# Hybrid decoder layer on one core: the last block pair of the second FFN and the final norm worked by token halves

## The reference, cut to what matters

```python
def rms_norm(x, gain):
    y = x * lax.rsqrt(jnp.mean(x * x, axis=-1, keepdims=True) + EPS)
    return y * gain
# one layer; x is (1, 512, 1024), D_FF is 2816
x = x + 0.5 * gate1 * swiglu(modulate(rms_norm(x, g0), ...), ffn1_w_in, ffn1_w_down)
x = x + gate2 * (merged @ w_out)        # merged: two chunked gated linear attentions
h = modulate(rms_norm(x, g2), ...)
gate, up = jnp.split(h @ ffn2_w_in, 2, axis=-1)
x = x + 0.5 * gate3 * ((silu(gate) * up) @ ffn2_w_down)
return rms_norm(x, final_norm)
```

## Time and profile before

| | us |
|---|---|
| median of 3 runs | 1282.38 (1280.68 to 1282.44) |
| the profiled execution | 1284.87 |
| its span, first to last instruction | 1283.1 |
| PE busy | 1229.7 (96%) |
| DVE, ACT, POOL busy | 600.7, 415.4, 86.4 |
| last matmul of the last pair ends, from the span's start | about 1269.1 |
| first output store issued | 1276.37 |

### The profile page before, as it was taken

How to read it: one execution, slowest core, us unless ns; L and a number is a source line. 1 busy time by engine, 2 the same in 40 slices (tenths; PEclk the granted TensorE clock), 3 DMA queues, 4 the chain that set the end, 5 groups by cost and what they waited for, 6 DMA issues and landing times.

```text
span 1283.1 us, 15169 instructions
## 1 busy us (share of the span) xinstructions
PE 1229.7 (96%) x6099; PEld 1017.7 (79%) x6099; DVE 600.7 (47%) x714; ACT 415.4 (32%) x442; POOL 86.4 (7%) x121
## 2 busy tenths in 40 slices
PE   3699999999999999999999999999999999999996
PEld 2578888888878997877887788888988888888885
DVE  6855555556343657566645233345523232332231
ACT  4522222222222355544344322233422222222222
POOL 5100000000000043022320000000000000000000
PEclk7799999999999999999999999999999999999998
DMA  9275556545352422121221133233222223222211
GB/s 379 67 244 172 180 172 196 191 157 168 123 180 99 132 66 66 36 64 36 66 66 45 55 99 99 94 103 99 66 81 93 88 98 98 98 90 87 94 58 65
DMA packets 119789, 143.40 MB, mean 112 GB/s; under 512 B 3892, under 2 KB 102336, under 8 KB 119744
## 3 DMA queue, kind: packets, MB, share of 16 engines
q1 hardware_dynamic: 119560, 142.69, 34.0%
q10 hardware_dynamic: 184, 0.07, 0.0%
HBM read 140.65 MB, written 2.10 MB: 111 GB/s over the span
## 4 chain that ended last, share of the span: by engine, by line
issue 49%; PE 37%; DVE 7%; ACT 3%; DMA 3%; POOL 1%; SPq 0%; ACTq 0%; POOLq 0%; DVEq 0%
PE PS L478 10%; PE PS L480 10%; PE PS L479 10%; PE PS L682 3%; DVE ACC L1300 2%; ACT WH L873 1%; PE PS L608 1%; PE PS L521 1%; DMA RAW<-in_ffn_w_down_dram 1%; DMA RAW<-in_w_in_mix_dram 1%; PE PS L523 1%; PE PS L522 1%; DMA RAW<-in_ffn_w_in_dram 1%; DVE WL L1200 1%; PE PS L722 1%
## 5 line engine op out<-in xcount | busy, mean ns | idle before, releaser
L478 PE MATMUL PS<-HH,WH 128*128 128x512 f32 (+1 forms) x1064 | 416.0, 391 | 7.4 <-DVE HL L1222 4.4
L480 PE MATMUL PS<-HH,WL 128*128 128x512 f32 (+1 forms) x1064 | 407.9, 383 | 0.0
L479 PE MATMUL PS<-HL,WH 128*128 128x512 f32 (+1 forms) x1064 | 407.6, 383 | 0.0
L1200 DVE TENSOR_TENSOR WL<-RAW,WH 128x2048 fp32r<-128x2048 f32 (+1 forms) x97 | 216.8, 2235 | 342.9 <-ACT WH L873 342.9
L873 ACT ACTIVATE WH<-RAW 128x2048 fp32r<-128x2048 f32 (+1 forms) x97 | 180.8, 1864 | 409.5 <-PE PS L480 370.8
L478 PEld LDWEIGHTS PS<-HH,WH 128*128 128x128 f32 x1064 | 201.1, 189 | 52.6 <-issue 6.8
L480 PEld LDWEIGHTS PS<-HH,WL 128*128 128x128 f32 x1064 | 201.1, 189 | 42.2
L479 PEld LDWEIGHTS PS<-HL,WH 128*128 128x128 f32 x1064 | 201.4, 189 | 40.5 <-issue 1.0
L478 PE MATMUL PS<-UH,WH 128*128 128x512 f32 (+1 forms) x372 | 140.3, 377 | 0.5 <-DVE WL L1200 0.5
L479 PE MATMUL PS<-UL,WH 128*128 128x512 f32 (+1 forms) x372 | 139.9, 376 | 0.0
L480 PE MATMUL PS<-UH,WL 128*128 128x512 f32 (+1 forms) x372 | 139.7, 375 | 0.0
(11 more groups left out here) (225 smaller groups left out, 1217.5 us busy)
## 6 DMA issues: line engine op xcount, KB each, us to landing
RAW<-in_ffn_w_in_dram SPq DMA_DIRECT2D x44, 1024.0 KB, 5.1
ADAW<-in_w_ada_dram SPq DMA_DIRECT2D x56, 512.0 KB, 5.7
RAW<-in_w_in_mix_dram SPq DMA_DIRECT2D x22, 1024.0 KB, 5.2
RAW<-in_ffn_w_down_dram SPq DMA_DIRECT2D x16, 1024.0 KB, 5.2
ADA<-in_w_ada_dram SPq DMA_DIRECT2D x8, 1024.0 KB, 13.7
RAW<-in_ffn_w_down_dram SPq DMA_DIRECT2D x7, 768.0 KB, 4.7
RAW<-in_w_out_dram SPq DMA_DIRECT2D x3, 1024.0 KB, 5.1
XST<-in_x_dram SPq DMA_DIRECT2D x4, 512.0 KB, 5.0
```

The source lines that it names most:

```text
L478: mm(ps, whi, ahi, start=start, stop=False)
L479: mm(ps, whi, alo, start=False, stop=False)
L480: return mm(ps, wlo, ahi, start=False, stop=stop)
L1200: V.tensor_tensor(WL[s][:, 0:size], RAW[s][:, 0:size], WH[s][:, 0:size].bitcast(F32), ALU.subtract)\
```

## The change

The last of the four pairs (feature blocks 6 and 7) is no longer done 512 tokens wide. Its matmuls are 256 wide, 264 of them, into four PSUM banks (`FIN_BANK`: banks 2 and 3 for the first token half, 6 and 7 for the second). In its first two units the halves alternate for each row block; in the third the order is first half block 6, first half block 7, second half block 6, second half block 7, and each of these four parts reports its end by itself (`quarter`, `last_done`).

What follows a part is done by halves too. DVE adds to `X` (`tail_add`), multiplies by the gain (`tail_gain`, done by ACT before) and adds block 6's squares to `S` (`tail_square`); ACT squares (`half_square`). PE's `tail_sums(th)` transposes the half's two token tiles of both blocks into the banks of `TAIL_BANK`, and sums the squares by products with ones: `S` (blocks 0 to 6) and then block 7's squares straight from `SG`. `tail_sums(0)` stands inside the third part, behind 4 of its 6 row blocks; `tail_sums(1)` behind everything.

ACT forms the inverse RMS of a half's two tiles by Ln and Exp (`tail_r`) in place of DVE's and POOL's two steps; for that it loads the Ln/Exp table once, between the second and third pair. Then ACT scales tile 0 (later 2) and DVE tile 1 (later 3), each in two instructions: 768 features in `OUTT`, and the last 256 read straight from the PSUM bank of the transposes. SP sends tiles 0 and 1 whole, then 768 features of tiles 2 and 3, then the remaining 256 features of each: six stores.

```diff
@@ block.sync
-            for t in range(TT):
-                sp.wait_ge(fin_v if t < 2 else fin_a, t % 2 + 1)
-                sp.dma_start(out[0, t * P:(t + 1) * P, :], OUTT[:, t, :]).then_inc(out_dma, 16)
+            HEAD = 6 * P
...
+            sp.wait_ge(fin_a, 2)
+            store(0, slice(0, D))
+            sp.wait_ge(fin_v, 2)
+            store(1, slice(0, D))
+            sp.wait_ge(fin_a, 3)
+            store(2, slice(0, HEAD))
...
+            sp.wait_ge(fin_v, 4)
+            store(3, slice(HEAD, D))
@@ block.gpsimd
-            pool.wait_ge(v_ready, 1)
-            nc.gpsimd.tensor_tensor(R4[:, :], V4[:, :], HALF4[:, :], ALU.pow).then_inc(r_ready, 1)
@@ block.tensor
+            for pair in range(3):
+                n = N_F2DOWN + 3 * pair
+                down_pair(n, pair % 2, n + 1, 28 + 2 * pair - 2, 1, untranspose(2 * pair - 2) if pair else None)
+
+            def tail_sums(th):
+                for b in (6, 7):
+                    pe.wait_ge(fin_y, 7 + b - 6 + 2 * th)
+                    if b == 6 and th == 0:
+                        pe.wait_ge(fin_ev, 6)
+                    for c in range(2):
+                        t = 2 * th + c
+                        ins = nc.tensor.transpose(PS[:, TAIL_BANK[th][c], (b - 6) * P:(b - 5) * P],
+                                                  YF[b % 2][:, t * P:(t + 1) * P], IDENT[:, :])
+                    ins.then_inc(fin_t, 1)
+                    if b == 6:
+                        pe.wait_ge(sacc, 31 + th)
+                        pe.wait_ge(xready, 28 + 7 + th)
+                    else:
+                        pe.wait_ge(sq_ready, 28 + 8 + 2 * th)
+                    for c in range(2):
+                        t = 2 * th + c
+                        src = S[:, t * P:(t + 1) * P] if b == 6 else SG[:, 1, t * P:(t + 1) * P]
+                        ins = mm(PS[:, 2 + th, c:c + 1], src, ONES[:, 0:1], start=b == 6 and c == 0, stop=b == 7 and c == 1)
+                ins.then_inc(ssq_done, 1)
...
+                    if piece == 2 and (th, m, k) == (1, 0, 4):
+                        tail_sums(0)
@@ block.scalar
+            exp_ln_tables()
+            down(N_F2DOWN, 1, 28, 23, final=True, qs=(0,))
...
+            def tail_r(th):
+                two = R4[:, 2 * th:2 * th + 2]
+                act.wait_ge(ssq_done, 6 + th)
+                A(two, PS[:, 2 + th, 0:2], ACT.Ln, bias=EPST[:, 0:1], scale=1.0 / D).then_inc(fin_ln, 1)
+                act.wait_ge(fin_ln, 1 + th)
+                A(two, two, ACT.Exp, scale=-0.5).then_inc(fin_r, 1)
...
+            half_square(6, 0, 28 + 7)
+            act.wait_ge(sacc, 23 + 7)
+            half_square(7, 0, 28 + 8)
+            half_square(6, 1, 28 + 9)
+            tail_r(0)
+            tail_scale(0)
+            half_square(7, 1, 28 + 10)
+            tail_r(1)
+            tail_scale(1)
@@ block.vector
+            dve.wait_ge(quarter, 7)
+            tail_add(6, 0)
...
+            dve.wait_ge(quarter, 9)
+            tail_add(6, 1)
+            tail_gain(6, 1)
+            tail_square(1)
+            dve.wait_ge(fin_ev, 6)
+            tail_scale(0)
+            dve.wait_ge(last_done, 3)
+            tail_add(7, 1)
+            tail_gain(7, 1)
+            tail_scale(1)
```

More of the change, by code:

```diff
@@ new lines, in _ @@
+            pe.wait_ge(xready, 28 + 4)
+            for piece in range(3):
+                n = N_F2DOWN + 9 + piece
+                pe.wait_ge(unit_lo, n + 1)
+                whi, wlo = weights(n)
+                nk = (DB, DB, FB - 16)[piece]
+                parts = [(th, m) for th in range(2) for m in range(2)]
+                steps = [(k, th, m) for k in range(nk) for th, m in parts] if piece < 2 else \
+                        [(k, th, m) for th, m in parts for k in range(nk)]
+                for k, th, m in steps:
+                    if piece == 2 and (th, m, k) == (1, 0, 4):
+                        tail_sums(0)
+                    w = slice(m * P, (m + 1) * P)
+                    ins = three(PS[:, FIN_BANK[th][m], half_t(th)], whi[:, k, w], wlo[:, k, w],
+                                UH[:, 8 * piece + k, half_t(th)], UL[:, 8 * piece + k, half_t(th)],
+                                piece == 0 and k == 0, piece == 2 and k == nk - 1)
+                    if piece == 2 and k == nk - 1:
+                        ins.then_inc(last_done if (th, m) == (1, 1) else quarter, 1)
+                if piece < 2:
+                    ins.then_inc(unit_done, 1)
+                if piece == 0:
+                    untranspose(4)()
@@ L854, in _ @@
+            tail_sums(1)
         @block.scalar
@@ L1171, in _, with tail_scale @@
             swiglu_in(N_F2IN, 1)
[L1172 to L1180, removed]
+            down(N_F2DOWN, 0, 28, 23, final=True)
+            exp_ln_tables()
+            down(N_F2DOWN, 1, 28, 23, final=True, qs=(0,))
+            n = N_F2DOWN + 9
+            split_hi(n + 2, raw_value(n + 2), n + 1, down_size(2))
+            final_copy(4)
+            final_copy(5)
+            def tail_r(th):
[4 more added lines that the diff above has]
+                A(two, two, ACT.Exp, scale=-0.5).then_inc(fin_r, 1)
+            def tail_scale(th):
+                t = 2 * th
+                act.wait_ge(fin_r, 1 + th)
+                A(OUTT[:, t, 0:6 * P], OUTT[:, t, 0:6 * P], ACT.Copy, scale=R4[:, t:t + 1]).then_inc(fin_a, 1)
+                act.wait_ge(fin_t, 8 + 2 * th)
+                A(OUTT[:, t, 6 * P:D], PS[:, TAIL_BANK[th][0], 0:2 * P], ACT.Copy, scale=R4[:, t:t + 1]).then_inc(fin_a, 1)
+            act.wait_ge(fin_ev, 6)
+            act.wait_ge(sacc, 23 + 6)
+            half_square(6, 0, 28 + 7)
[7 more added lines that the diff above has]
+            tail_scale(1)
         @block.vector
@@ L1564, in _ @@
             clear_s()
[L1565 to L1573, removed]
+            down(N_F2DOWN, 0, 2, 28, 24, 2)
@@ new lines, in _ @@
+            dve.wait_ge(quarter, 7)
+            tail_add(6, 0)
+            dve.wait_ge(fin_t, 6)
+            tail_gain(6, 0)
+            tail_square(0)
+            dve.wait_ge(quarter, 8)
+            tail_add(7, 0)
+            tail_gain(7, 0)
+            dve.wait_ge(quarter, 9)
[6 more added lines that the diff above has]
+            tail_add(7, 1)
```

40 lines of the change are left out of this document (33 added, 7 removed).

## The result

The changed kernel takes 1268.24 us (median; runs from 1266.76 to 1269.58), the kernel before in the same comparison 1282.41 (1280.68 to 1283.79): a ratio of 0.9888, interval 0.9874 to 0.9901. That is 14.2 us faster, where 3.9 had been forecast, and far outside the range. The profiled executions have spans of 1267.9 and 1283.1 us, 15.3 apart.

The account below looks back on a forecast made before the run. PE, busy 96%, was left alone; the end was bound by a 7.4 us chain to the first store, then 5.0 us of full DMA. +1.0 +1.3 -3.8 -2.4 gave -3.9 us, median 1278.5, range 1277.0 to 1280.5.

Parts of the forecast that it names:

- The step that failed: Matmuls ahead of the last pair: PE, busy 96% of the span, left alone by the change, so nothing gained there.
- The tail's sum: Last pair to span's end: +1.0 and +1.3 on PE, -3.8 in the chain, -2.4 in the stores, together -3.9 us.
- PE, forecast +2.3: Last pair on PE: 264 half-width matmuls cost +0.98 us, tail_sums(0) inside the stream 1.3; last part ends issuing 2.3 later.
- rival A: Tail: clock falls or PE waits in tail_sums(0), 0.6 to 1.05 us; gain only 2.8 to 3.3 us; chance 0.18.
- The chain from there to the first store of the end: Behind the last matmul: last issue to second half's first store takes 3.6 us in place of 7.4.
- The last addition: DVE behind the last matmul: ready at 1271.46 but queued behind the first half's scaling, 0.2 us lost.
- The clock: PE's last sums: idle only about 0.7 us before, so full clock; other bound 0.6 us slower in sums and transposes together.
- The stores: Output: first half's transfer just hidden, second half at 419 and 391 GB/s; -2.4 us, span ends at 1279.2.
- the sign of being wrong that asked for over 3 us: End of the stores: forecast wrong if the last landing came over 3 us behind the last issue.
- Rival B: Stores: last small store lands 3.6 to 4.7 us behind its issue; gain only 2.9 to 1.8 us; chance 0.14.
- Rival C: SP's store issues back up, over 1.1 us each from the third; span ends at 1283.4, 0.3 late; chance 0.03.
- Rival D: Tail: ACT and DVE overlap more, DVE's scaling does not delay the last addition; 1277.5 to 1278.0 us; chance 0.13.

Follow-up runs that it names:

- old_arena_m64: Kernel before with only V4 and HALF4 moved behind the arena, so the arena starts at 89792 in place of 89856: 1273.29 us, ratio 0.9927.
- new_arena_0: Changed kernel with V4 and HALF4 declared again, unused, so the arena starts at 89856 as before: 1278.92 us, ratio 0.9967.
- old_arena_p64: Kernel before with V4 and HALF4 behind the arena and an unread 32-element tile ahead of it, arena at 89920: 1283.66 us.
- tail_scale_late: Changed kernel with the first half's inverse RMS and scaling moved behind the second half's addition, gain and square: 1269.98 us, tail 43.29 us.
- tail_four_stores: Changed kernel with tiles 2 and 3 sent whole, four stores of 512 KB in place of six: 1272.12 us, tail 41.62 us.

## Why the prediction was wrong, by its own steps

**The step that failed** is the first: "The change leaves that part alone; every instruction up to the third pair of the last product stays". The instructions stayed; the addresses of their operands did not, and I took the pace of the matmuls ahead of the last pair as given, a change of 0. The mean gap of 512-wide ones sank from 232.4 to 229.0 ns, and the last pair starts 11.0 us earlier, of 15.3 between the spans. old_arena_m64 shows it alone, new_arena_0 takes it out: there the change measures 3.7 us (2.3 to 6.3), with 3.9 forecast. None of the rivals named it. The busy shares could not have told it. The starts of the matmuls in a row could have raised the question, with one gap in seven of 238 ns or more on an engine that waits for nothing, but not answered it: old_arena_p64 is slower still and has hardly any such gap.

**The tail's sum** came out at -4.2 us against -3.9, in part by luck, as the yardstick below shows. By its terms, each counted as the prediction counts it, from the start of the transposes behind the last matmul (the end of its issue):

- PE, forecast +2.3: from the pair's first matmul to there it is 33.27 us (1226.39 to 1259.66), before 31.55, so +1.7; with the addresses alike +2.1 at the old ones (new_arena_0, 1237.16 to 1270.79) and +2.2 at the new (against old_arena_m64, 31.09). The 96 matmuls up to the transposes took 0.118 us each (1237.70 - 1226.39 over 96), forecast 0.120. tail_sums(0) took 1.2 us (1255.54 to 1256.74), forecast 1.3, and PE did not wait in it: rival A's wait, and the bound of the earlier trace rows, did not come.
- The chain from there to the first store of the end, forecast 3.6 us in place of 7.4: 3.66 (1259.66 to 1263.32, the third issue). The last addition is late behind DVE's scaling by 0.23 us, forecast 0.2. Square, gain, transposes and sums follow as forecast, and from Ln's start to scaling it is 0.53 us (1261.83 to 1262.36), forecast 0.5:

```profile
1260.09 0.47 DVE L1645 SCALAR_TENSOR_TENSOR X<-PS,GATE,X 128x256 f32<-128x256 f32 x1
1260.41 5.21 SPq L393 DMA_DIRECT2D out_dram<-OUTT  x6
1260.60 0.42 ACT L951 ACTIVATE SG<-X 128x256 f32<-128x256 f32 x1 [0.21 <-DVE X L1645]
...
1261.01 0.44 PE L865 MATMUL PS<-IDENT,YF 128*128 128x128 f32 x2 [0.63 <-DVE YF L1650]
1261.29 0.50 PE L876 MATMUL PS<-ONES,SG 128*128 128x1 f32 x4
1261.83 0.26 ACT L1233 ACTIVATE R<-PS,EPST 128x2 f32<-128x2 f32 x1 [0.81 <-PE PS L876]
1262.12 0.20 ACT L1235 ACTIVATE R<-R 128x2 f32<-128x2 f32 x1
1262.36 0.94 ACT L1240 ACTIVATE OUTT<-OUTT,R 128x768 f32<-128x768 f32 x1
```

- The clock: granted 1.00 up to 1261.80 and so through the last sums, which take 0.50 us, as those of the first half do; PE had stood idle 0.63 us, forecast 0.7. That part of rival A fell too.

```profile
1255.00:1261.80 6.80, 6.16 (x54) 5.99 (x53) 3.22 (x8) 2.81 (x7) 0.00 (x0) 1.00 0.08 33
```

But the yardstick was off. In old_arena_m64, whose tail has the instructions of before, the same sums ran at the full clock, after the same 2.25 us of idle time (the start of its last pair, the transposes behind its last matmul, then the end):

```profile
1221.23 0.39 PE L478 MATMUL PS<-UH,WH 128*128 128x512 f32 x1
...
1252.32 0.60 PE L837 MATMUL PS<-IDENT,YF 128*128 128x128 f32 x4
1255.17 0.63 PE L837 MATMUL PS<-IDENT,YF 128*128 128x128 f32 x4 [2.25 <-ACT OUTT L1014]
1255.63 0.95 PE L850 MATMUL PS<-ONES,S 128*128 128x1 f32 x8
```

Against 0.92 and 1.71 us in the earlier trace rows. From the end of the last matmul's issue to the end of the span it is 13.3 us there (1252.32 to 1265.66), in before's profiled execution 14.1; in the other eight runs with that tail, at eight other pairs of addresses and at every pace of the table, 13.15 to 13.36. So 0.8 us of the 4.2 are the one execution's early fall of the clock, and 0.5 the faster pace inside the last pair (31.55 us in before, 31.09 in old_arena_m64). Tail against tail the change is worth 3.0 us at the changed kernel's address (44.43 against 41.46). The forecast of 3.9 had the 0.8 in it, in the chain's -3.8, so without it the sum says 3.1. I had read a term of the sum off a single execution, and it was the unusual one of ten.

- The stores, forecast 4.3 us from the second half's first issue to the end in place of 6.75: 4.54. What the issues and landings were, by the line of SP's stores, against the earlier trace rows:

```profile
L393 SPq DMA_DIRECT2D out_dram<-OUTT x6: 332/428/943, 1260.4 to 1264.7; - x6
...
DMA to landing us min/median/max: 2.3/2.9/3.5
```

From the last issue to the end of the span it is 3.2 us (1264.68 to 1267.86), forecast 3.0; the last store landed 2.8 us behind its issue, at 1267.46, so the sign of being wrong that asked for over 3 us did not show. Rival B had 3.6 at least and fell. Rival C wanted issues of over 1.1 us from the third on; the longest took 0.94, and SP was done 2.2 us ahead of the end. (In tail_scale_late, where the stores are issued closer together, the fourth took 1.20.) (C's sum also counts the 3.6 us from the end of the last issue, where the earlier trace rows count from its start; put right it ends at 1282.3, not slower than before.) The DMA engines while stores of 512, then 384, then 128 KB moved:

```profile
1262.00:1263.80 1.80, 0.00 (x0) 0.00 (x0) 1.01 (x2) 1.59 (x4) 0.00 (x0) 0.55 1.02 405
1264.20:1266.00 1.80, 0.00 (x0) 0.00 (x0) 0.00 (x0) 0.00 (x0) 0.00 (x0) 0.50 1.02 394
1266.30:1267.00 0.70, 0.00 (x0) 0.00 (x0) 0.00 (x0) 0.00 (x0) 0.00 (x0) 0.50 0.93 312
```

They move 405, 394 and 312 GB/s, where four stores of 512 KB had 419; the prediction took 419 and 391, and the slower last pieces would account for the 0.2 us that the stores took longer (not tested apart). The first half's data end at 1264.03 and the second's start at 1264.15, so the first half was just hidden, as forecast. The Trainium skill, "DMA: Bandwidth & Descriptors", section "Rules for kernel authors", wants 1 MiB or more per DMA for the most bandwidth. The smaller pieces are indeed slower here, 312 GB/s at 128 KB against 405 at 512 KB, but with whole tiles (tail_four_stores) the tail was 0.16 us longer, so the rule does not decide in this place.

Rival D (more overlap, DVE's scaling does not delay the last addition) fell: the addition is 0.23 us late.

## What to carry to other kernels

Whoever adds or drops a small buffer moves all that is allocated behind it; compare the addresses of moving operands and weights before and after, and measure the edit once with the old layout kept, or a gain of the layout is booked on the code. Where matmuls run without a wait, take the mean gap of their starts, not their busy time: with some 4000 in this kernel 3 ns each are 12 us, and padding costs one line. Which distance is best has to be tried for the kernel at hand, since only this one was measured. And what a single execution shows of the clock near the end is to be checked on a second before it becomes a term of a sum.

## What the runs showed of the hardware that was not expected

- The 512-wide matmuls of this kernel start every 227.2 ns when moving operands and weights lie a multiple of 256 bytes apart in the partition, every 229.0 to 229.1 when 64 over, and every 232.4 to 233.3 at 32, 96, 128 and 192 over (table above), at a granted clock of 1.00. Runs with the same residue at other addresses agree to 0.1 ns, except at 128 (232.4 to 232.8). Ten pairs of addresses were run; two distances a multiple of 256 apart were compared once, at 64 over. What resource is shared was not shown; nor whether WH alone, WL or the input tiles RAW, which move with them, set the distance.
- The 256-wide matmuls of the same traces do not follow it in the same order (mean of gaps under 150 ns): 119.8 ns at 0, 115.9 to 117.2 at 64, 119.1 to 119.3 at 128, 116.3 at 192.
- After the same 2.25 us of idle time PE's last sums ran at a granted clock of 0.51 (1.2 of 2.4 GHz) in one execution and of 1.00 in nine others with the same instructions.
